# Early queries, keys and biases for the first pair of heads, and reciprocals ahead of the second half of the scores

## The chip, the cores and the metric

The kernel runs on one NeuronCore of one Trainium2 chip. The metric is the device time of one execution in microseconds (us); less is better. The core's engines are TensorE (PE in the profile; its weight loads are PEld), VectorE (DVE), ScalarE (ACT), GpSimd (POOL) and SyncE (SP), which here only issues transfers. Each engine works through its own instructions in order, and they wait for one another through semaphores.

## What is computed

One inference step of a two-layer decoder trunk, for a prompt of 1024 tokens and 8 sample tokens, width 1024. The change touches layer 0 alone: its input projection and the attention behind it.

```python
def even_project(h, pos, w_in, ...):
    z = h @ w_in                      # six sections of 512 columns, and 8 forget logits
    qa, ka = rms_norm(heads(z[..])), rms_norm(heads(z[..]));  va = heads(z[..])
    logf = log_sigmoid(z_forget + b_f)
    qb, kb = partial_rope(rms_norm(..)), partial_rope(rms_norm(..));  vb = heads(z[..])

def fox_block(q, c_q, k, v, c_k):     # group A, 8 heads of 64
    s = q @ k.T * SCALE + (c_q - c_k)     # c = cumsum(logf)
    s = where(pos_k <= pos_q, s, -inf)
    return softmax(s) @ v

# group B, 8 heads: the same over keys at dilations 1, 4, 16, mixed by softmax denominators
# the samples: the same against cached keys, values and log-forgets
# then x += concat(A, B) @ w_out;  x += swiglu(rmsnorm(x));  layer 1 (gated chunk mixing);  x += swiglu(..)
```

## The kernel before, in words

**Projection.** `in_pe` runs `step(i)` for the two head groups i = 0 (A) and i = 1 (B); each has three sections c = 0, 1, 2 for queries, keys and values, and each section nine tiles of tokens (one of 8 sample tokens, eight of 128 prompt tokens). A tile is 24 products of 512 columns into one of three PSUM banks (0 to 2). VectorE scales it out of the bank, and ScalarE's queue stores it to memory (`q_prompt`, `k_prompt`, `v_prompt`; line 739). `step(0)` is written out and `step(1)` stands in a loop of one turn (`peeled_loop`).

**Between.** `forget_pe` (lines 965 to 967) makes the sample tokens' bias sums with three products into banks 2 to 4, and `forget_dve` turns them into `dbias` with a chain of 17 small VectorE operations (lines 945 to 950); it also clears `L`, `Lp` and `Ls` and makes the causal mask tiles `ident16` and `above16`. TensorE and ScalarE wait for the end of that chain (`lg` 14).

**Attention.** The 16 heads are taken as 8 pairs; a pair has 8 units, one for each block of 128 queries, the longest (8 blocks of keys) first: 64 units in all. For each pair, queries and keys come from memory in four parts (`load_qk`, line 997; part n belongs to pair n/4), and TensorE turns each with four 128x128 transposes (`transpose_qk`, line 1229); ScalarE copies even parts and VectorE odd ones to `QT` and `KTr`. The parts of the first pair (n = 0 to 3) are loaded and transposed after the projection, into banks 0 to 3; those of the next pairs within the units before (`QK_AT`), into bank 7.

The order within the attention is written out by hand in `att_pe`, `att_act` and `att_dve`, for u from -2 on. TensorE's turn u is: scores of unit u+2, first half (`scores(u+2, 0)`, line 1246; for group A with two small products of the mask, line 1250); the sums of unit u spread over the rows (`spread_sums`, line 1277, which reads `rl` = 1/l); the product with the values (`window`, line 1293); transposes of the weights of unit u+1 (line 1265), a part of the next pair, scores of u+2, second half, more transposes. VectorE's turn is: bias and minimum of unit u+2's first half (`biased`, line 1453), the output of unit u (`out`, line 1468), one sum of products for the sample tokens (`log_sum`, line 1480), `biased` of the second half, `reciprocals(u+1)` (line 1461), a second `log_sum`. ScalarE takes the exponentials (line 1369) and copies the transposed weights (line 1382).

**The transfer queue.** SyncE issues nearly all loads in one order, in `att_begin_sp` and `att_sp`: parts 0 to 2, `hmask`, `dbias`, part 3, the biases of the first pair (`load_first_bias`), the sample queries `qrep`, six tiles of cached keys `kring`, the values of the first pair `vp`, `own`, then parts 4 to 6. All of them share SBUF with the projection's weight units (`raw`, `Wh`, `Wl`).

The few lines that set this order on SyncE:

```python
sp.wait_ge(z_ps, 2 * NZT)                       # att_begin_sp: the whole projection is done
for j in range(NZ):
    sp.wait_ge(z_out[j], 16 * 2 * NZT // NZ)    # and all of it is stored
for n in range(3):
    load_qk(sp, n)
```

## Time and profile before

| | us |
|---|---|
| median of 3 runs | 2630.19 |
| the runs | 2628.05 to 2633.60 |
| the profiled execution | 2626.38 |
| its span in the profile | 2624.3 |
| TensorE busy, of the span | 2556.8 (97%) |
| VectorE, ScalarE, GpSimd busy | 1133.9, 550.1, 1101.6 |
| last product of the projection starts | 345.83 |
| first scores start | 359.66 |
| last scores biased | 681.12 |

Times within the profile count from the start of its span. The profile gives for each instruction its start and length, and before it the engine's idle time with what ended it; the granted clock of TensorE is given for a stretch, 1.00 for 2.4 GHz and 0.50 for 1.2 GHz. Transfers are listed by their issue and by the time from issue to landing.

### The profile page before, as it was taken

Reading aid. Unit: us, or ns where it says so; the run is one execution under the profiler, and the core shown is the slowest. Engines: PE = TensorE matmul, PEld = TensorE weight load, DVE = VectorE, ACT = ScalarE, POOL = GpSimd, SP = SyncE. Lnnn points to the kernel's source line nnn. Section 1 sums busy time; section 2 is a strip of 40 time slices with the busy share of each in tenths; the row PEclk is TensorE's granted clock in tenths of the full one; section 3 lists DMA queues with packets and bytes.
Section 4 is the critical chain, followed back from the end, with each engine's and each line's share of the span. In section 5 each row is a group of like instructions: output and inputs, shape, how many; then the busy total and the mean of one; then the engine's idle time right before and its main releaser. Section 6 shows DMA issues by size and latency. Waiting matters only on the chain.

```text
span 2624.3 us, 42745 instructions
## 1 busy us (share of the span) xinstructions
PE 2556.8 (97%) x16331; PEld 2344.0 (89%) x16331; DVE 1133.9 (43%) x2258; ACT 550.1 (21%) x1266; POOL 1101.6 (42%) x702
## 2 busy tenths in 40 slices
PE   7999989999999999999999999899999999999999
PEld 5777756666899999999999987899999999999999
DVE  6636536667344333333333360553733333333333
ACT  5201136666322000000000051322300000000001
POOL 4234115566665444333344262435654443333440
PEclk9999999999999999999999999999999999999999
DMA  5223148767312111111111111111121111111111
GB/s 158 70 80 91 60 129 247 217 203 211 96 34 73 49 43 45 44 44 48 48 48 48 33 49 32 49 33 49 33 65 48 44 43 45 43 48 48 48 32 65
DMA packets 218459, 189.83 MB, mean 72 GB/s; under 512 B 29443, under 2 KB 171523, under 8 KB 217956
## 3 DMA queue, kind: packets, MB, share of 16 engines
q1 hardware_dynamic: 200996, 161.89, 21.2%
q10 hardware_dynamic: 17344, 26.35, 2.8%
q8 instruction: 75, 1.23, 0.2%
q14 instruction: 44, 0.36, 0.0%
HBM read 171.19 MB, written 17.01 MB: 72 GB/s over the span
## 4 chain that ended last, share of the span: by engine, by line
PE 69%; DVE 2%; POOL 2%; ACT 1%; issue 1%; ACTq 0%; POOLq 0%; PEldq 0%; DVEq 0%
PE ps L536 63%; PE ps L566 1%; PE ps L568 1%; PE ps L567 1%; ACT ps L2079 1%; POOL Xl L509 1%; POOL Wl L392 1%; POOL Wh L389 1%; DVE hs L479 0%; PE ps L2042 0%; POOL acc_sq L450 0%; PE ps L1265 0%; PE ps L1293 0%; PE ps L2211 0%; DVE VM_EARLY L2163 0%
## 5 line engine op out<-in xcount | busy, mean ns | idle before, releaser
L536 PE MATMUL ps<-Xh,Wh 128*128 128x256 f32 (+2 forms) x2712 | 872.6, 322 | 9.7 <-PE ps L536 3.3
L536 PE MATMUL ps<-Xl,Wh 128*128 128x256 f32 (+2 forms) x2712 | 867.4, 320 | 0.0
L536 PE MATMUL ps<-Xh,Wl 128*128 128x256 f32 (+2 forms) x2712 | 866.4, 319 | 0.0
L389 POOL TENSOR_TENSOR Wh<-raw,zeros 128x1024 fp32r<-128x1024 f32 x178 | 353.9, 1988 | 1072.5 <-PE ps L536 782.4
L536 PEld LDWEIGHTS ps<-Xh,Wh 128*128 128x128 f32 x2712 | 510.3, 188 | 15.6 <-issue 8.8
L536 PEld LDWEIGHTS ps<-Xh,Wl 128*128 128x128 f32 x2712 | 510.9, 188 | 0.0
L536 PEld LDWEIGHTS ps<-Xl,Wh 128*128 128x128 f32 x2712 | 510.3, 188 | 0.7
L392 POOL TENSOR_TENSOR Wl<-raw,Wh 128x1024 fp32r<-128x1024 f32 x178 | 440.9, 2477 | 14.0
L1839 DVE TENSOR_TENSOR Hl<-hf,Hh 128x392 fp32r<-128x392 f32 (+1 forms) x132 | 181.8, 1377 | 464.8 <-ACT Hh L1775 464.8
L536 PE MATMUL ps<-Hh,Wh 128*128 128x392 f32 (+2 forms) x1056 | 340.7, 323 | 1.2 <-DVE xT L1848 1.2
L536 PE MATMUL ps<-Hl,Wh 128*128 128x392 f32 (+2 forms) x1056 | 338.1, 320 | 0.0
L536 PE MATMUL ps<-Hh,Wl 128*128 128x392 f32 (+2 forms) x1056 | 336.8, 319 | 0.0
L1848 DVE TENSOR_TENSOR xT<-ps,xT 128x392 f32<-128x392 f32 (+2 forms) x528 | 263.1, 512 | 163.5 <-PE ps L536 160.6
L1767 ACT ACTIVATE sg<-ps 128x392 f32<-128x392 f32 (+1 forms) x132 | 60.4, 458 | 1062.2 <-PE ps L536 1062.1
L566 PE MATMUL ps<-Wh,Xh 128*128 128x512 f32 x512 | 204.2, 399 | 9.1 <-DVE zt L859 4.0
L1837 DVE TENSOR_TENSOR hf<-ps,sg 128x392 f32<-128x392 f32 (+1 forms) x132 | 67.2, 509 | 320.6 <-PE ps L536 316.5
L568 PE MATMUL ps<-Wh,Xl 128*128 128x512 f32 x512 | 203.2, 397 | 0.0
L567 PE MATMUL ps<-Wl,Xh 128*128 128x512 f32 x512 | 202.8, 396 | 0.0
L536 PEld LDWEIGHTS ps<-Hh,Wh 128*128 128x128 f32 x1056 | 199.0, 188 | 1.7 <-DVE xT L1848 1.4
L536 PEld LDWEIGHTS ps<-Hh,Wl 128*128 128x128 f32 x1056 | 199.5, 189 | 0.0
L536 PEld LDWEIGHTS ps<-Hl,Wh 128*128 128x128 f32 x1056 | 199.5, 189 | 0.0
L1194 POOL TENSOR_TENSOR kring<-kring,qrep 128x512 f32<-128x512 f32 (+1 forms) x96 | 120.6, 1274 | 95.6 <-DMA qrep<-q_sample 60.7
(251 smaller groups left out, 2485.9 us busy)
## 6 DMA issues: line engine op xcount, KB each, us to landing
raw<-in_w_gate_up SPq DMA_DIRECT2D x88, 512.0 KB, 3.8
raw<-in_w_down SPq DMA_DIRECT2D x44, 512.0 KB, 3.5
kring<-in_cache_a_k SPq DMA_DIRECT2D x64, 256.0 KB, 3.6
ring<-in_cache_a_v SPq DMA_DIRECT2D x64, 256.0 KB, 3.1
raw<-in_w_in_even SPq DMA_DIRECT2D x20, 512.0 KB, 4.1
raw<-in_w_in_c SPq DMA_DIRECT2D x16, 512.0 KB, 3.9
xs<-in_x_prompt SPq DMA_DIRECT2D x8, 512.0 KB, 8.5
q_prompt<-zt ACTq DMA_DIRECT2D x16, 256.0 KB, 2.0
```

What stands on the lines that cost most here:

```text
L389: pool.tensor_tensor(h[:, :], r[:, :], zeros[:, :].to_broadcast([P, 1024]), ALU.add).then_inc(split_high, 1)
L392: pool.tensor_tensor(l[:, :], r[:, :], h[:, :].bitcast(F32), ALU.subtract).then_inc(split_done, 1)
L509: eng.tensor_tensor(Xl[:, m, c0:c0 + n], hs[u % NH][:, 0:n], Xh[:, m, c0:c0 + n].bitcast(F32), ALU.subtract).then_inc(s["low_dve" if m % 2 ...
L536: ins = nc.tensor.matmul(out, w, x, start=(j == 0), stop=(j == len(pairs) - 1))
L566: nc.tensor.matmul(out, xh, h, start=begin, stop=False)
L567: nc.tensor.matmul(out, xh, l, start=False, stop=False)
L568: return nc.tensor.matmul(out, xl, h, start=False, stop=end)
L1194: pool.tensor_tensor(keys, keys, qrep[0:r, g, :], ALU.mult).then_inc(prod_done, 1)
L1767: act.activation(sg[:, k % NB, 0:w], ps[:, gate_bank(i, is_last, k), 0:w], ACT.Silu).then_inc(f["silu"].sem, 1)
L1837: dve.tensor_tensor(hf[:, k % NB, 0:w], ps[:, bank, 0:w], sg[:, k % NB, 0:w], ALU.mult).then_inc(f["hid"].sem, 1)
L1839: dve.tensor_tensor(Hl[:, t, c0:c0 + w], hf[:, k % NB, 0:w], Hh[:, t, c0:c0 + w].bitcast(F32), ALU.subtract).then_inc(f["low"].sem, 1)
L1848: dve.tensor_tensor(x, ps[:, jobs.index(("dn", b, m, 0)) % 6, 0:w], x, ALU.add).then_inc(f["dn_add"].sem, 1)
```

## The change

1. **Homes.** `QT` moves to the first raw buffer, parts n = 0 and 1 (`qk_pair`) to the second, and biases, keys, `qrep`, `KTr` and the rest to buffers of split weights that the last section of the projection no longer uses. `bias` has its two halves in two buffers.
2. **The first pair within the projection.** In the last section (i = 1, c = 2), after its tiles 4 to 7, TensorE transposes parts 0 to 3 into banks 3 to 6, and ScalarE and VectorE copy them. SyncE loads parts 0 and 1 as soon as the last keys are stored, then the biases, then parts 2 and 3 as banks are transposed. `step(1)` is written out too, on TensorE, ScalarE and VectorE.
3. **The forget sums.** The three products of `forget_pe` move behind the scores of unit 0, into banks 5 to 7, and VectorE's chain between `biased(1, 0)` and `reciprocals(0)`. `ustr` and `lnd` are made in the last section, the mask tiles right behind the last tile. TensorE's waits for `lg` move to the first places where a bank or `dbias` matters.
4. **The queue.** Behind the projection SyncE issues `hmask`, `dbias`, the values of the first pair, `qrep`, the six keys, `own`, parts 4 to 6.
5. **Reciprocals.** `reciprocals(u + 1)` stands ahead of the first `log_sum` and of `biased(u + 2, 1)`.
6. **The end of the attention.** The raw buffers now hold `QT` and `qk_pair`: of the output projection's weights (units 25 on) only unit 25 is loaded at once, units 26 on after the last scores have been biased.

```diff
@@ homes
+        QT = at_unit("QT", RAW_AT, [P, SEQ])
+        qk_pair = at_unit("qk_pair", RAW_AT + 1, [P, 2, 2 * 2 * P])
...
+        bias = at_unit("bias", HIGH_AT + 2, [P, SPL, SEQ])[:, 0:SPL:SPL - 1, :]
...
@@ in_pe, in_act, in_dve
+        def early_pair(i, c, pos):
+            return pos - 4 if (i, c) == (1, 2) and 4 <= pos < 8 else None
+                        if early_pair(i, c, tt) is not None:
+                            transpose_qk(pe, 0, early_pair(i, c, tt), 3 + early_pair(i, c, tt))
-            peeled_loop(pe, 2, step)
+            for i in range(2):
+                step(i)
...
+                        if early_pair(i, c, pos) in (0, 2):
+                            copy_queries_keys(act, 0, early_pair(i, c, pos), 3 + early_pair(i, c, pos))
...
+                            if (i, pos) == (1, 2):
+                                forget_operands(dve)
+                            if early_pair(i, c, pos) in (1, 3):
+                                copy_queries_keys(dve, 0, early_pair(i, c, pos), 3 + early_pair(i, c, pos))
@@ forget_pe
-            pe.wait_ge(z_free, 2 * NZT)
-            nc.tensor.matmul(ps[:, 2, :], ustr[:, :], flat, start=True, stop=True)
+            nc.tensor.matmul(ps[:, 6, :], ustr[:, :], flat, start=True, stop=True)
...
@@ SyncE
+        def att_early_sp(sp):
+            sp.wait_ge(split_done, 25)
+            for j in range(NZ):
+                sp.wait_ge(z_out[j], 16 * (NZT + 2 * TT) // NZ)
+            for n in range(2):
+                load_qk(sp, n)
+            sp.wait_ge(z_ps, NZT + 2 * TT)
+            sp.wait_ge(c_out, 16)
+            for part in range(3):
+                load_first_bias(sp, part)
+            for n in range(2, 4):
+                load_qk(sp, n)
         def att_begin_sp(sp):
...
-            for n in range(3):
-                load_qk(sp, n)
...
-                load_qk(sp, 3)
                 for part in range(3):
-                    load_first_bias(sp, part)
+                    load_pair_values(sp, 0, part)
                 for g in range(2):
                     load_queries(0, g)
                 for j in range(KR):
                     load_key(0, j)
-                for part in range(3):
-                    load_pair_values(sp, 0, part)
                 own_sp(sp)
@@ att_pe
+                if u == 0:
+                    pe.wait_ge(z_free, 2 * NZT - 1 + c)
...
+                    if y == 1:
+                        pe.wait_ge(lg, 6)
...
-            for g in range(4):
-                transpose_qk(0, g, g)
-            pe.wait_ge(lp_zero, 2)
...
+                if u == -2:
+                    forget_pe(pe)
@@ att_dve
+                if u == -1:
+                    forget_dve(dve)
...
+                reciprocals(u + 1)
                 tiles = log_tiles(u)
                 for sample, tile in tiles[0:1]:
                     log_sum(sample, tile)
                 biased(u + 2, 1)
-                reciprocals(u + 1)
@@ SyncE, behind the attention
-            load_narrow(sp, BASE_OUT, a["w_out_even"][0], 8)
+            load_narrow(sp, BASE_OUT, a["w_out_even"][0], 0, 1)
+            sp.wait_ge(s_biased, 2 * chunk_base[NUNIT])
+            load_narrow(sp, BASE_OUT, a["w_out_even"][0], 1, 8)
```

**TensorE at the end of the projection.** Before, its last product (line 568) is followed by the forget products, the four parts and the first scores:

```order
L89 COMPARE_AND_BRANCH
L965 MATMUL ps<-lfp_56,ustr_199 128x512 [waits z_ps,z_free,lg,lfp_in]
L966 MATMUL ps<-lfp_56,ones_50 128x512
L967 MATMUL ps<-lnd_200,ones_50 128x64
L1229 MATMUL ps<-ident_49,qk0_148 128x128 [waits qk_in0,lg]
L1229 MATMUL ps<-ident_49,qk0_148 128x128 x3
L1229 MATMUL ps<-ident_49,qk1_149 128x128 [waits qk_in1]
...
L1229 MATMUL ps<-ident_49,qk2_179 128x128 [waits qk_in2]
...
L1246 MATMUL ps<-KTr_160,QT_153 128x512 [waits qk_dve,qk_act,lp_zero]
...
L1250 MATMUL ps<-ident16_165,above16_166 128x128 x2
```

With the change each of tiles 4 to 7 has a part behind it (here the last one, part 3, and the first product of tile 8), and behind tile 8 stand the scores at once; the next part (4) keeps its place in unit 0's turn:

```order
L574 MATMUL ps<-Wh0_65,Xl_62 128x512
L1263 MATMUL ps<-ident_49,qk_pair_149 128x128 [waits qk_in0]
L1263 MATMUL ps<-ident_49,qk_pair_149 128x128 x3
L572 MATMUL ps<-Wh3_68,Xh_61 128x512 [waits z_free]
...
L574 MATMUL ps<-Wh0_65,Xl_62 128x512
L1294 MATMUL ps<-KTr_159,QT_148 128x512 [waits z_ps,z_free,qk_dve,qk_act]
...
L1299 MATMUL ps<-ident16_162,above16_163 128x128 [waits lp_zero]
...
L1294 MATMUL ps<-KTr_159,QT_148 128x512 [waits z_free,qk_dve,qk_act]
...
L988 MATMUL ps<-lfp_56,ustr_195 128x512 [waits lg,lfp_in]
L989 MATMUL ps<-lfp_56,ones_50 128x512
L990 MATMUL ps<-lnd_196,ones_50 128x64
L1294 MATMUL ps<-KTr_159,QT_148 128x384 [waits s_biased]
```

What moved: sixteen transposes into the last section, three forget products behind the scores of unit 0.

**SyncE between the projection and the attention** (`kring` are cached keys of the samples, `c_dram` holds the biases). Before:

```order
L997 DMA qk0_148<-q_prompt 128x2x128 [waits z_out1,z_out2,z_out0,z_ps]
L997 DMA qk0_148<-out_k_prompt 128x2x128
...
L1006 DMA hmask_184<-in_c_hmask 128x10
L1007 DMA dbias_182<-in_c_dbias 128x8x32
L997 DMA qk0_148<-q_prompt 128x2x128 [waits qk_ps,c_out]
...
L1102 DMA bias_152<-c_dram 128x2x512
...
L1146 DMA qrep_159<-q_sample 128x512 x2
...
L1090 DMA kring0_150<-in_cache_a_k 128x512
...
L1120 DMA vp_156<-out_v_prompt 128x4x128
...
L1013 DMA own_181<-out_v_sample 8x512 [waits own_zero]
```

With the change, parts 0 to 3 and the biases stand ahead of `hmask`, and the values ahead of the queries and keys:

```order
L1024 DMA qk_pair_149<-q_prompt 128x2x128 [waits z_out1,z_out2,z_out0,split_done]
L1024 DMA qk_pair_149<-out_k_prompt 128x2x128
...
L1140 DMA bias_155<-c_dram 128x2x512 [waits c_out,z_ps]
...
L1024 DMA qk_pair_149<-q_prompt 128x2x128 [waits qk_ps]
...
L1024 DMA qk_pair_149<-q_prompt 128x2x128 [waits qk_ps]
...
L1045 DMA hmask_181<-in_c_hmask 128x10 [waits z_out1,z_out2,z_out0,z_ps]
L1046 DMA dbias_179<-in_c_dbias 128x8x32
L1158 DMA vp_156<-out_v_prompt 128x4x128
...
L1184 DMA qrep_153<-q_sample 128x512 x2
...
L1128 DMA kring_home0_150<-in_cache_a_k 128x512
...
L1051 DMA own_178<-out_v_sample 8x512 [waits own_zero]
```

What moved: 8 loads of parts and 3 of biases to before the projection's end, 3 of values past 2 of `qrep` and 6 of keys; parts 4 to 6 stand last as before.

**VectorE in turn u = 6** (`mx` is the minimum that the exponential waits for). Before:

```order
L1468 TENSOR_TENSOR O2_175<-ps,Rs0_163 128x128 [waits o_low,pv_ps,pt_out]
L1480 TENSOR_REDUCE L_183<-kring0_150 128x8 [waits prod_done]
L1453 ISA S2_00_157,mx_186<-ps,bias_odd_192,mx_tail_187 128x512 [waits pt_ps,s_biased,s_ps,bias_in0]
L1453 ISA mx_186 128x1
L1453 ISA S2_10_158,mx_186<-ps,bias_odd_192,mx_tail_187 128x512 [waits s_biased]
L1453 ISA mx_186 128x1
L1461 RECIPROCAL rl_189<-lsum_188 128x2 [waits p_done]
L1480 TENSOR_REDUCE L_183<-kring1_151 128x8 [waits prod_done]
```

With the change the reciprocal stands ahead of the first sum and of the second half:

```order
L1513 TENSOR_TENSOR O2_172<-ps,Rs0_160 128x128 [waits o_low,pv_ps,pt_out]
L1506 RECIPROCAL rl_186<-lsum_185 128x2 [waits p_done]
L1519 TENSOR_REDUCE L_180<-kring_home0_150 128x8 [waits prod_done]
L1498 ISA S2_00_157,mx_183<-ps,bias_odd_188,mx_tail_184 128x512 [waits pt_ps,s_biased,s_ps,bias_in0]
...
L1498 ISA S2_10_158,mx_183<-ps,bias_odd_188,mx_tail_184 128x512 [waits s_biased]
...
L1519 TENSOR_REDUCE L_180<-kring_home0_150 128x8 [waits prod_done]
```

What moved: the reciprocal past one sum and two operations of line 1453 (line 1498 in the changed kernel).

## Rows read from the trace of the kernel before

**Rows 1.** Stretch: length, busy of PE, PEld, DVE, ACT, POOL, clock, DMA share, GB/s.

```profile
346.20:375.20 29.00, 18.25 (x108) 10.84 (x108) 12.84 (x52) 9.32 (x19) 1.22 (x3) 0.82 0.78 205
```

**Rows 2.** TensorE's timeline, 345 to 376 us: start, length, instruction, idle before.

```profile
345.83 0.39 PE L568 MATMUL ps<-Wh,Xl 128*128 128x512 f32 x1
...
354.27 2.82 PE L1229 MATMUL ps<-ident,qk 128*128 128x128 f32 x12 [4.12 <-DVE acc L950]
...
359.66 2.08 PE L1246 MATMUL ps<-KTr,QT 64*128 64x512 f32 x4
...
372.52 1.97 PE L1293 MATMUL ps<-PT,vp 128*64 128x128 f32 x32 [0.94 <-DMA vp<-out_v_prompt]
...
375.23 0.60 PE L1229 MATMUL ps<-ident,qk 128*128 128x128 f32 x4
```

**Rows 3.** The timeline of SyncE's queue, 349 to 370 us.

```profile
349.41 0.37 SPq L997 DMA_DIRECT2D qk<-q_prompt  x1
...
352.89 0.68 SPq L1007 DMA_DIRECT2D dbias<-in_c_dbias  x1
...
358.16 0.94 SPq L1146 DMA_DIRECT2D qrep<-q_sample  x2
359.89 6.29 SPq L1090 DMA_DIRECT2D kring<-in_cache_a_k  x6
366.22 1.68 SPq L1120 DMA_DIRECT2D vp<-out_v_prompt  x3
...
368.72 0.39 SPq L997 DMA_DIRECT2D qk<-q_prompt  x1
369.15 0.47 SPq L997 DMA_DIRECT2D qk<-out_k_prompt  x1
```

**Rows 4.** TensorE's waits, 366 to 690 us: total, times, longest.

```profile
PE ps L1277 <- DVE rl L1461: 8.5, 12, 2.3
```

**Rows 5.** Timelines of ScalarE's queue and VectorE, 306 to 325 us.

```profile
306.88 0.34 ACTq L739 DMA_DIRECT2D out_k_prompt<-zt  x1
...
324.12 0.75 DVE L841 TENSOR_SCALAR zt<-ps,rstd 128x512 f32<-128x512 f32 x1 [4.63 <-PE ps L568]
```

**Rows 6.** Transfers of key parts, issued 369.1 and 375.8 us on: median us to landing.

```profile
qk<-out_k_prompt SPq DMA_DIRECT2D x1, 128.0 KB, 5.2
...
qk<-out_k_prompt SPq DMA_DIRECT2D x1, 128.0 KB, 2.3
```

**Rows 7.** Stretches, with the columns of rows 1.

```profile
263.90:267.20 3.30, 3.30 (x10) 2.56 (x9) 2.09 (x8) 1.24 (x3) 0.00 (x0) 0.50 0.47 179
...
352.70:362.30 9.60, 6.51 (x24) 4.08 (x26) 2.97 (x13) 1.32 (x4) 0.00 (x0) 0.50 0.76 194
...
365.00:370.00 5.00, 2.82 (x19) 1.90 (x20) 1.76 (x7) 4.25 (x8) 0.00 (x0) 1.00 1.00 349
```

**Rows 8.** VectorE's timeline, 350 to 355 us.

```profile
350.88 0.22 DVE L945 TENSOR_SCALAR acc<-ps 128x64 f32<-128x64 f32 x1
...
354.00 0.21 DVE L950 TENSOR_TENSOR acc<-ps,acc 128x64 f32<-128x64 f32 x1
```

**Rows 9.** Timelines of the three engines around a pair's first unit, 402 to 406 us.

```profile
402.61 1.15 ACT L1369 ACTIVATE S<-S,mx 128x1024 f32<-128x1024 f32 x1 [0.67 <-DVE mx L1453]
...
403.37 0.44 PE L1277 MATMUL ps<-ident,rl 128*64 128x128 f32 x4 [0.68 <-DVE rl L1461]
...
403.96 1.09 PE L1265 MATMUL ps<-ident,S 128*128 128x128 f32 x8
...
404.03 1.14 ACT L1369 ACTIVATE S<-S,mx 128x1024 f32<-128x1024 f32 x1
...
404.93 0.28 DVE L1468 TENSOR_TENSOR O<-ps,Rs 128x128 f32<-128x128 f32 x1
```

**Rows 10.** Timelines of VectorE and GpSimd at the attention's end.

```profile
681.12 0.29 DVE L1453 CUSTOM_DVE_ANT_0 S<-ps,dist 128x128 f32<-128x128 f32 x1
...
689.47 1.90 POOL L389 TENSOR_TENSOR Wh<-raw,zeros 128x1024 fp32r<-128x1024 f32 x1
```

More of the change, by code:

```diff
@@ L234, in build, with at_unit @@
         NO = 4
-        qk = [place(f"qk{j}", [P, 2, 2, P]) for j in range(2)]
-        kring = [place(f"kring{j}", [P, DH]) for j in range(2)]
-        bias_memory = used[0]
-        bias = place("bias", [P, 2, SEQ])
-        QT = place("QT", [P, SEQ])
-        kring += [place(f"kring{j}", [P, DH]) for j in range(2, 4)]
-        vp = place("vp", [P, 8, P])
-        S2 = [[None, None], [None, None]]
-        S2[0][0] = place("S2_00", [P, SEQ])
-        S2[1][0] = place("S2_10", [P, SEQ])
-        qrep = place("qrep", [P, 2, DH])
-        KTr = place("KTr", [P, SEQ])
-        kring += [place(f"kring{j}", [P, DH]) for j in range(4, 6)]
+        def at_unit(name, buffer, shape, dt=F32):
+            return nc.alloc_sbuf_tensor_at(name, shape, dt, offset=(overlay + 31) // 32 * 32 + 4 * 1024 * buffer)
+        RAW_AT, HIGH_AT, LOW_AT = 0, RAW, RAW + SPL
+        QT = at_unit("QT", RAW_AT, [P, SEQ])
+        qk_pair = at_unit("qk_pair", RAW_AT + 1, [P, 2, 2 * 2 * P])
+        qk = [qk_pair[:, j, :].rearrange("p (x t e) -> p x t e", x=2, t=2) for j in range(2)]
+        kring_home = [at_unit(f"kring_home{j}", b, [P, 2, DH]) for j, b in enumerate((HIGH_AT, HIGH_AT + 3, LOW_AT + 3))]
+        kring = [kring_home[j // 2][:, j % 2, :] for j in range(KR)]
+        qrep = at_unit("qrep", HIGH_AT + 1, [P, 2, DH])
+        dist = at_unit("dist", HIGH_AT + 2, [P, SEQ])
+        bias = at_unit("bias", HIGH_AT + 2, [P, SPL, SEQ])[:, 0:SPL:SPL - 1, :]
+        assert HIGH_AT + 2 + SPL - 1 == LOW_AT + 1
+        vp = at_unit("vp", HIGH_AT + 4, [P, 8, P])
+        S2 = [[None, None], [None, None]]
+        S2[0][0] = at_unit("S2_00", HIGH_AT + 5, [P, SEQ])
+        S2[1][0] = at_unit("S2_10", LOW_AT, [P, SEQ])
+        KTr = at_unit("KTr", LOW_AT + 2, [P, SEQ])
+        used[0] = (overlay + 31) // 32 * 32 + 4 * 1024 * (LOW_AT + 4)
         Rs = [place(f"Rs{j}", [P, P]) for j in range(2)]
@@ L251, in build @@
         used[0] += 4 * P
-        score_memory = used[0]
         S2[0][1] = place("S2_01", [P, SEQ - P])
@@ L256, in build @@
         O = [place(f"O{j}", [P, P]) for j in range(NO)]
+        mv_memory = used[0]
         MV = place("MV", [P, DH])
         vx = place("vx", [P, 2, P])
-        qk.append(place("qk2", [P, 2, 2, P]))
+        qk.append(place("qk2", [P, 2, 2, P])[:, :, :, :])
         ring = place("ring", [P, SLOTS, DH])
@@ L282, in build @@
         assert used[0] <= lfp_end
-        used[0] = score_memory
+        used[0] = mv_memory
         ustr = place("ustr", [P, P])
@@ L337, in load_wide, with load_narrow @@
                 load_unit(sp, base + j, j + (base % SPL if isinstance(base, int) else 0), rows(w, 2 * j, 2, col, DH), 2)
-        def load_narrow(sp, base, w, count):
-            for m in range(count):
+        def load_narrow(sp, base, w, first, end):
+            for m in range(first, end):
                 load_unit(sp, base + m, base + m, rows(w, 0, KT, m * P, P), KT)
@@ L810, in in_act @@
             input_square(act, 2)
-            peeled_loop(act, 2, step)
+            for i in range(2):
+                step(i)
         def in_dve(dve):
@@ L880, in in_dve @@
             input_low(dve, 1)
-            peeled_loop(dve, 2, step)
+            for i in range(2):
+                step(i)
         lg, lg_a = sem("lg"), sem("lg_a")
@@ L951, in forget_dve @@
             dve.wait_ge(lg, n)
+            dve.wait_ge(lf_out, 32)
+            dve.memset(Lp[:, :, :], 0.0).then_inc(lp_zero, 1)
+            dve.memset(L[:, :, :], 0.0)
+            dve.memset(Ls[:, :], 1.0)
         def forget_act(act):
@@ L996, in load_qk @@
                 for x, src in enumerate((q_prompt, a["k_prompt"])):
-                    sp.dma_start(qk[n % 3][:, x, :, :], src[grp, rows, cols].rearrange("(t p) e -> p t e", p=P)).then_inc(qk_in[n % 3], 16)
+                    sp.dma_start(queries_keys(n)[:, x, :, :], src[grp, rows, cols].rearrange("(t p) e -> p t e", p=P)).then_inc(qk_in[n % 3], 16)
+        def att_early_sp(sp):
[10 more added lines that the diff above has]
+                load_qk(sp, n)
         def att_begin_sp(sp):
@@ L1546, in after_window @@
                     gathered(sample_at(w, VALUES_AT + 2), w)
-            for g in (1, 3):
-                copy_queries_keys(0, g, g)
-            dve.wait_ge(att_const_in, 32)
             for u in range(-2, NUNIT):
```

99 lines of the change are left out of this document (49 added, 50 removed).

## The prediction

> **What bounds the kernel now.** I read the profile from the whole to the seam. TensorE is busy nearly all of the span, so only a stretch in which it stands still, or runs at half its clock, can give time back. The table of stretches shows one: from the end of the projection to the fifth part's transposes it is busy 18.25 of 29.0 us, at a mean clock of 0.82 [rows 1]. TensorE's timeline shows what stands there [rows 2]. The last product ends at 345.83 + 0.39 = 346.2. The transposes of the first parts begin at 354.27, after 4.12 us without work, and the first scores only at 359.66. At 372.52 the values of the first pair were late by 0.94 us. At 375.23 come the transposes of part 4, and from there on TensorE's waits are few. So 375.23 is my landmark: how much earlier it comes is the gain at the seam. SyncE's queue shows what is behind it [rows 3]: nothing of the attention is issued before 349.41, when the last store has landed. Then SyncE needs until 369 for everything up to part 4. Within the attention the largest of TensorE's waits is for the reciprocals, 12 times, 8.5 us together [rows 4]. That wait is what the change's second half is about.
>
> **The first pair within the projection.** Removed from the seam are sixteen transposes, their loads, the copies and the biases. They cost TensorE something in the last section, which it fills without a gap. Twelve of them took 2.82 us at half clock [rows 2, 7], so four would take 0.47 at full clock, and four within the attention 0.60 [rows 2]. I take 0.53 for each part, 2.1 us for four, with bounds 1.9 and 2.4. The projection then ends at 346.2 + 2.1 = 348.3. Are the parts there in time? The last keys' store is issued at 306.88 and the fifth tile is scaled from 324.12 on [rows 5]. That leaves 17 us for a store and for a load that lands within 5.2 us [rows 6]. Parts 2 and 3 are issued when parts 0 and 1 are transposed and are wanted two tiles later, some 11 us, since VectorE's row for a tile is 0.75 long behind 4.63 of waiting; that suffices too. The copies lie beside projection tiles, on engines that wait for them. Writing out `step(1)` removes a few register and branch instructions from engines of which TensorE shows no idle time there: nothing.
>
> **The landmark without a late transfer.** From the first scores to the landmark took 375.23 - 359.66 = 15.6 us, of which 0.9 was the wait for the values. With the scores starting at 348.3 that puts it at about 363. The forget sums now lie in this stretch: 3 products, and on VectorE the chain from 350.88 to 354.21, 3.3 us [rows 8], ahead of the second half of unit 1. That half used to wait for TensorE for about as long, and the first scores save about 1 us at full clock. I let these cancel. If they don't, the next paragraph hides them: it is later than 363 in any case.
>
> **What is late next: part 4.** SyncE issues the loads of part 4 behind the values, `qrep` and six keys, as before, and the only thing that has left the queue ahead of them is what now comes early. Counted from the projection's end: the last store lands after 349.41 - 346.2 = 3.2 us; `hmask` and `dbias` take 1.2 (the row of `dbias` ends at 353.57, and 0.5 more is `hmask`), `qrep` 359.89 - 358.16 = 1.7, the keys 366.22 - 359.89 = 6.3, values and `own` together 368.72 - 366.22 = 2.5, and the key half of part 4 is issued 0.4 later [rows 3]. That is 15.3. Such a transfer took 5.2 us to land where 1 MB of biases and all the keys were queued before it, and 2.3 on a quiet queue [rows 6]. The biases are gone, and keys are issued at 256 KB in 1.05 us, 250 GB/s, where the queues moved 349 [rows 7]. So I take 3.0, near the lower end. Part 4 is there at 348.3 + 15.3 + 3.0 = 366.6, and TensorE, ready at 363, waits some 3.7 us for it. The seam gives 375.23 - 366.6 = **8.6 us**, where without that wait it would give 12. By the fit of 2.0 us plus bytes over 436 GB/s in the Trainium skill (DMA: Bandwidth & Descriptors, Anatomy of one DMA), made for another issuing path, my estimate is 2.3 us for these 128 KB; the gain would be 0.7 larger. The quiet row agrees with it and the loaded row does not, which is why I go by the rows.
>
> **The clock.** After a wait of 1.9 us in the projection TensorE worked 3.3 us at 0.50 [rows 7]; work of 3.3 us at half clock is worth 1.6. After the long wait at the seam now it was 9.6 us at 0.50 with 6.5 busy, a loss of 3.3, and a stretch of 5 us that was busy for 2.82 kept 1.00 [rows 7]. A new wait of 3.7 us is nearest to the first in what follows it, dense work: I take a loss of **1.6**, between 0 and 3.3.
>
> **The reciprocals.** The wait of 0.68 at 403.37 is typical: `rl` was late because VectorE biased the second half first. With `rl` early TensorE goes on 0.7 sooner, but its next work but one, the transposes at 403.96, needs the exponential that started at 402.61, right behind VectorE's minimum, and takes until about 403.85 with its readout [rows 9]. So the wait moves one step down, from `rl` to the exponential. On VectorE the same work stands ahead of that minimum, plus a reciprocal of 0.16, which at eight pair starts may cost 1.3 us. The two longest waits (2.3 the longest [rows 4]) have the same end: VectorE was waiting there for GpSimd's product, and the minimum waits for it still. A few small waits in other units remain as gain. I take **0.3** together, between -1.3 and 8.5.
>
> **The end of the attention.** Unit 26 is loaded once the last scores are biased, at 681.4, and GpSimd splits it only at 689.47, behind its own last outputs [rows 10]. That leaves 8 us for a transfer: nothing. If it were late, its split and then TensorE would be late by what is missing.
>
> **Sum.** 8.6 - 1.6 + 0.3 = 7.3 us less. Against the profiled execution of 2626.38 that is 2619.1; the median of the runs shown stands 3.8 higher at 2630.19, and what is timed is compared with it: **2622.9 us**.
>
> **Rivals.**
> - *The reciprocals pay.* If the moved waits find work that is ready, up to all 8.5 us come on top of 7.0: 2630.2 - 15.5 = 2614.7 at best, 2618 with half of it. For it: 12 waits on just this operation. Against it: the exponential in rows 9 ends 0.1 us before TensorE wants it. Chance 0.12.
> - *The queue is as full as before.* Then part 4 takes 5.2 us to land (2.2 more) and the clock costs 3.3: 8.6 - 2.2 - 3.3 + 0.3 = 3.4 us, 2626.8, no difference that can be told. For it: values and `qrep`, 1 MB, are issued within 3.5 us right ahead of the keys. Against it: the biases' 1 MB is gone. Chance 0.21.
> - *The reciprocal blocks VectorE: slower.* It waits for the exponential of the second head. At 404.03 + 1.14 and its readout this ends at about 405.3, while the output ahead of it starts at 404.93 and is over by 405.2 [rows 9]: everything behind it, the second half's bias and the sums of the samples, would stand for 0.1 to 0.3 us. If that happened in every unit at 0.3, and TensorE felt it, it would be 64 x 0.3 = 19 us, less 7.0: 12 slower, 2642. It decides from 0.11 us a unit on. Against it: the row is of a pair's first unit, where the window is shortest and the exponential longest; elsewhere the window covers the exponential. A wait at the head of VectorE's queue holds all behind it by the Trainium skill too (TensorE: Matmul & The Clock Gate, Architectural detail: strictly first in, first out). Chance 0.05.
> - *The change does not do what it says:* the order of instructions shows that it does; what could fail is only the timing of the early loads, for which there are 17 us.
>
> **How the numbers follow.** The measurement can tell about 0.2%, 5.3 us, from no change. My forecast, a gain of 5.3 to 9, has a chance of 0.6; its own range is 2620 to 2625. With the first rival that makes 0.71 for faster. The second rival and the forecast's lower edge make 0.24 for no difference, the third 0.05. The range from 2616.5 to 2627.5 reaches from half of the first rival to the second, and leaves out the slower case.
>
> **What would show it.** Right: the first scores within 0.5 us of the projection's end, four transposes behind each of tiles 4 to 7 with no wait for `qk`; a wait of 3 to 5 us ahead of the transposes of part 4 with the transfer of `qk` as what ended it, the clock at 0.50 for some us behind it; TensorE's wait for `rl` nearly gone, and in its place waits for exponentials (line 1369 now) of about the same sum. Wrong: part 4 in time (gain near 12), waits for `rl` gone and none in their place, VectorE waiting for exponentials at each reciprocal, or GpSimd waiting for the weights of unit 26.

## The result, and the profile after

| | kernel before | changed kernel |
|---|---|---|
| median of 5 runs | 2630.21 us (2628.05 to 2633.6) | 2618.39 us (2611.99 to 2618.64) |
| profiled execution | 2626.38 us, span 2624.3 | 2618.45 us, span 2616.6 |
| granted clock, mean of the profiled execution | 0.992 | 0.994 |

The ratio is 0.9947, with a 95% interval from 0.9932 to 0.9961. The changed kernel is faster by 11.8 us between the medians (13.9 by the ratio). I had forecast 7.3. The time lies inside the range, near its fast edge; the gain is over half as large again as I said. Between the two profiled executions it is 7.9 us.

**The seam.** TensorE's timeline of the changed kernel, 345.5 to 372 us: start, length, instruction, idle before.

```profile
346.27 0.39 PE L574 MATMUL ps<-Wh,Xl 128*128 128x512 f32 x1
346.96 1.13 PE L1294 MATMUL ps<-KTr,QT 64*128 64x512 f32 x4 [0.30 <-PE ps L574]
...
353.98 0.65 PE L1316 MATMUL ps<-ident,S 128*128 128x128 f32 x4 [0.83 <-DVE acc L964]
...
359.93 0.98 PE L1316 MATMUL ps<-ident,S 128*128 128x128 f32 x7
365.86 1.11 PE L1263 MATMUL ps<-ident,qk_pair 128*128 128x128 f32 x4 [4.95 <-DMA qk_pair<-out_k_prompt]
366.90 2.08 PE L1294 MATMUL ps<-KTr,QT 64*128 64x512 f32 x4
368.91 1.75 PE L1316 MATMUL ps<-ident,S 128*128 128x128 f32 x7
```

The first scores follow the projection's last product after 0.30 us, where 13 us lay between them before [rows 2]. Then all is dense until 360.9, but for 0.83 at 353.98 and 0.25 at 357.81. There TensorE stands 4.95 us for part 4, the wait that the prediction named. Behind it four transposes take 1.11 instead of 0.60, four scores 2.08 instead of 1.13: it works at half its clock.

The stretches of the changed kernel, columns as in rows 1: from the last product to part 4, behind part 4, and the place in the projection that rows 7 show at 0.50 before.

```profile
346.66:365.86 19.20, 12.87 (x91) 7.20 (x92) 10.89 (x47) 9.13 (x16) 4.38 (x6) 0.98 0.73 198
364.90:371.70 6.80, 5.84 (x23) 3.25 (x23) 1.43 (x4) 2.25 (x5) 0.00 (x0) 0.51 0.31 87
258.00:270.00 12.00, 10.14 (x45) 7.93 (x44) 10.10 (x22) 2.26 (x5) 2.67 (x2) 1.00 0.39 116
```

The same twelve microseconds of the projection in the kernel before:

```profile
258.00:270.00 12.00, 10.15 (x38) 7.86 (x37) 10.11 (x22) 2.25 (x5) 2.46 (x1) 0.86 0.36 110
```

In front of the seam nothing differs but this: the same busy time, once at 1.00 and once at 0.86 in the mean, which is 1.7 us. The change does not touch that place, and this difference is chance: in a second profiled execution of each kernel it is the other way round, 1.00 before and 0.86 with the change (the same window of before_again and of after_again):

```profile
258.00:270.00 12.00, 10.07 (x44) 7.85 (x43) 10.11 (x22) 2.25 (x5) 2.47 (x1) 1.00 0.37 110
258.00:270.00 12.00, 10.07 (x37) 7.75 (x36) 10.14 (x18) 2.25 (x5) 3.77 (x2) 0.86 0.48 131
```

Of the 14 profiled executions of this study eight have 0.86 there and six 1.00.

The timeline of SyncE's queue in the changed kernel, 345 to 372 us:

```profile
349.83 0.34 SPq L1045 DMA_DIRECT2D hmask<-in_c_hmask  x1
...
351.06 1.71 SPq L1158 DMA_DIRECT2D vp<-out_v_prompt  x3
352.81 0.94 SPq L1184 DMA_DIRECT2D qrep<-q_sample  x2
354.56 5.82 SPq L1128 DMA_DIRECT2D kring_home<-in_cache_a_k  x6
...
361.16 0.40 SPq L1024 DMA_DIRECT2D qk_pair<-q_prompt  x1
361.60 0.47 SPq L1024 DMA_DIRECT2D qk_pair<-out_k_prompt  x1
```

The key half of part 4 is issued 14.9 us behind the projection's end (346.66) and is there 4.3 us later, at 365.86.

**The attention.** TensorE's waits of the changed kernel, 346 to 700 us: total, times, longest.

```profile
PE ps L1316 <- ACT S L1421: 5.2, 6, 2.2
PE ps L1263 <- DMA qk_pair<-out_k_prompt: 5.0, 1, 5.0
...
PE ps L1350 <- DVE Lm L1532: 2.1, 2, 1.4
...
PE ps L1328 <- DVE rl L1506: 0.6, 2, 0.3
```

The wait for `rl` is down from 8.5 us in 12 places [rows 4] to 0.6 in 2, and waits for exponentials (`S`) of 5.2 stand in its place; before there was one of 2.4, at the seam. At the pair's first unit, which is that of rows 9, it looks like this (timelines of ScalarE and of TensorE, 394 to 400 us):

```profile
395.83 1.15 ACT L1421 ACTIVATE S<-S,mx 128x1024 f32<-128x1024 f32 x1 [0.72 <-DVE mx L1498]
```

```profile
395.78 0.44 PE L1328 MATMUL ps<-ident,rl 128*64 128x128 f32 x4
...
397.12 1.09 PE L1316 MATMUL ps<-ident,S 128*128 128x128 f32 x8 [0.69 <-ACT S L1421]
```

The 0.68 has moved one step down, as 0.69. The transposes start at 397.12 and before at 403.96: 6.84 us have been won by here. The last wait of the attention, 0.30 us ahead of a product of the output projection, ends at 687.93 now and at 697.06 before, 9.13 earlier. So the rest of the attention adds 2.3 us. Behind it the difference falls to 7.7 at the span's end, over stretches at half clock that lie elsewhere in the two executions.

### The profile page after: what moved, and what is told of

The parts are those of the page before. It is cut to its first block, busy times and chain, and to the rows that moved or that the text cites. A ratio compares the mean times of both kernels' runs of the same rounds, so it can differ in the third digit from the quotient of the medians.

```text
span 2616.6 us, 42737 instructions
## 1 busy us (share of the span) xinstructions
PE 2554.6 (98%) x16331; PEld 2341.8 (89%) x16331; DVE 1130.3 (43%) x2258; ACT 551.1 (21%) x1266; POOL 1100.8 (42%) x702
## 4 chain that ended last, share of the span: by engine, by line
PE 71%; DVE 2%; POOL 2%; ACT 1%; issue 1%; DMA 0%; SPq 0%; ACTq 0%; POOLq 0%; PEldq 0%; DVEq 0%
PE ps L542 64%; PE ps L572 1%; PE ps L574 1%; PE ps L573 1%; PE ps L1294 1%; PE ps L1316 1%; PE ps L1346 1%; ACT ps L2119 1%; POOL Xl L515 1%; POOL Wl L398 1%; POOL Wh L395 1%; DVE hs L485 0%; PE ps L2082 0%; POOL acc_sq L456 0%; PE ps L1384 0%
## 5 line engine op out<-in xcount | busy, mean ns | idle before, releaser
L1229 POOL TENSOR_TENSOR kring_home<-kring_home,qrep 128x512 f32<-128x512 f32 (+1 forms) x96 | 120.6, 1273 | 95.1 <-DMA qrep<-q_sample 63.1
```

The costliest lines, as they stand in the source:

```text
L1229: pool.tensor_tensor(keys, keys, qrep[0:r, g, :], ALU.mult).then_inc(prod_done, 1)
```

## The experiments

Twelve runs were made, ten with an edit and two of the kernels as they stand. Each median stands beside that of the kernel before on the same chip in the same hour; a ratio of 0.001 is 2.6 us.

| run | median us | before | ratio, 95% interval |
|---|---|---|---|
| after_again | 2616.95 | 2630.17 | 0.9950 (0.9937 to 0.9964) |
| recip_back | 2620.67 | 2630.17 | 0.9966 (0.9952 to 0.9979) |
| recip_only | 2624.15 | 2630.17 | 0.9980 (0.9971 to 0.9989) |
| part4_early | 2609.96 | 2630.17 | 0.9922 (0.9909 to 0.9936) |
| loops_only | 2629.76 | 2630.10 | 1.0001 (0.9992 to 1.0010) |
| forget_first | 2615.33 | 2630.10 | 0.9943 (0.9929 to 0.9956) |
| sums_behind | 2605.62 | 2630.10 | 0.9910 (0.9896 to 0.9923) |
| forget_first_queue | 2614.96 | 2628.60 | 0.9945 (0.9932 to 0.9959) |
| recip_starts | 2615.51 | 2628.60 | 0.9946 (0.9932 to 0.9959) |
| sums_behind_recip_back | 2610.74 | 2628.60 | 0.9929 (0.9916 to 0.9943) |
| values_behind | 2617.24 | 2628.39 | 0.9962 (0.9948 to 0.9975) |
| before_again (one execution) | 2626.35 | | |

### What the reciprocals give

**recip_only** is the kernel before with one line moved:

```
                 if u >= 0 and QK_AT.get(j) in (1, 3) and it < PAIRS - 1:
                     copy_queries_keys(it + 1, QK_AT[j], 7)
+                reciprocals(u + 1)
                 tiles = log_tiles(u)
...
                 biased(u + 2, 1)
-                reciprocals(u + 1)
```

> The kernel before with only the reciprocals moved ahead of the second half of scores. Theory: 2 to 3 us faster than before, at the same first landmark (part 4's transposes at about 375 us), the waits for rl gone and those for exponentials in their place. Rival: within 0.5 us of before. If it is faster by 5 us or more, the first pair's part of the change gave less than its landmark says.

It is 6.0 us faster than before, twenty times the 0.3 that I had put down for this part. **recip_back** is the changed kernel with the opposite edit.

> The changed kernel with the reciprocals of 1/l back behind the second half of scores, everything else kept. Theory (the 2.3 us that the attention gained behind the first pair are the reciprocals' doing): 2 to 3 us slower than the changed kernel, the waits of TensorE for rl back to 8 to 9 us, and those for the exponential shorter. Rival 1 (my prediction's term): 0.3 us slower, the same within what is measured. Rival 2 (the gain behind the first pair is the clock's and the keys' order): no slower at all.

It is 3.7 us slower than the changed kernel beside it (2616.95). Both went the theory's way, and beyond its 2 to 3 us; the rival that stood for my own term fell. The 6.0 of recip_only met the condition that would have made the first pair's part smaller than its landmark, and that conclusion does not hold: recip_back, which is that part alone, is 9.5 us faster than before. The two parts overlap. Alone they give 6.0 and 9.5, together 13.2, and the 2.3 between are near the 2.1 us by which the early reciprocals lengthen the wait for part 4 (below). TensorE's waits, 346 to 700 us, of recip_only:

```profile
PE ps L1265 <- ACT S L1369: 7.3, 6, 2.6
...
PE ps L1297 <- DVE Lm L1491: 2.1, 2, 1.4
...
PE ps L1277 <- DVE rl L1461: 0.5, 2, 0.3
```

and of recip_back:

```profile
PE ps L1328 <- DVE rl L1506: 10.6, 13, 2.2
PE ps L1263 <- DMA qk_pair<-out_k_prompt: 2.9, 1, 2.9
...
PE ps L1350 <- DVE Lm L1532: 1.0, 2, 0.6
```

Before, the waits for `rl`, `S` and `Lm` made 8.5 + 2.4 + 1.0 = 11.9; in recip_only they make 0.5 + 7.3 + 2.1 = 9.9. Another 0.8, waits of the `rl` transposes for ScalarE's copy in the same view of before, is gone as well: 2.8 us less. With the change it is 10.6 + 1.0 + 0.8 = 12.4 against 0.6 + 5.2 + 2.1 = 7.9, of which 2.1 only come back in the wait for part 4 (5.0 for 2.9): 2.4 less. So the waits account for 2.4 to 2.8 us of the 3.7 to 6.0.

The longer waits for `Lm` are moved waits too. In the kernel before TensorE waits 0.68 for `rl` at 484.40 and 0.62 for `Lm` at 485.68, in recip_only 1.38 for `Lm` alone at 487.20; at the other place 0.23 and 0.40 became 0.70. Each time some 0.07 us is new.

Where I went wrong shows at one of the pairs' starts. Timelines of ScalarE and TensorE of the kernel before, 646 to 653 us:

```profile
649.42 1.15 ACT L1369 ACTIVATE S<-S,mx 128x1024 f32<-128x1024 f32 x1 [1.39 <-DVE mx L1453]
650.47 0.18 ACT L1369 ACTIVATION_READ_ACCUMULATOR S<-S,mx 128x1 f32 x1
```

```profile
650.18 0.44 PE L1277 MATMUL ps<-ident,rl 128*64 128x128 f32 x4 [1.63 <-DVE rl L1461]
650.45 0.39 PE L1293 MATMUL ps<-PT,vp 128*64 128x128 f32 x4
650.77 1.05 PE L1313 MATMUL ps<-hmask,MV 128*128 128x2 f32 x8
651.68 1.07 PE L1265 MATMUL ps<-ident,S 128*128 128x128 f32 x8
```

and TensorE at the same place of recip_only:

```profile
648.73 0.44 PE L1277 MATMUL ps<-ident,rl 128*64 128x128 f32 x4
648.99 0.39 PE L1293 MATMUL ps<-PT,vp 128*64 128x128 f32 x4
649.31 1.05 PE L1313 MATMUL ps<-hmask,MV 128*128 128x2 f32 x8
651.01 1.09 PE L1265 MATMUL ps<-ident,S 128*128 128x128 f32 x8 [0.64 <-ACT S L1369]
```

Here eight products of a sample (0.9 us) stand between the window and the transposes. So before, the exponential was over at 650.65, 1.03 us ahead of the transposes at 651.68. With `rl` early TensorE does those products while the exponential runs, and 1.63 of waiting becomes 0.64, 0.99 less. At rows 9 only the sums and the window, 0.59 us, stand there; the exponential was over 0.11 ahead of the transposes, and the wait stayed (0.68, 0.69). At the longest wait, 2.30 at 566.38, it was over at 566.85 for transposes at 566.96, and 2.38 is left. So what can be won at a place is the time by which the next thing waited for was already there. I had read the case of rows 9 and laid it on all the others.

**recip_starts** keeps the reciprocals early only around a pair's start:

```
+                if u % 8 in (6, 7):
+                    reciprocals(u + 1)
                 tiles = log_tiles(u)
...
                 biased(u + 2, 1)
+                if u % 8 not in (6, 7):
+                    reciprocals(u + 1)
```

> The changed kernel with the reciprocals ahead of the second half only in the two units around each pair's start, and behind it in the other six. Theory (at a pair's start the wait moves from rl to the exponential and little is gained; the gain of the reciprocals sits in the waits of 0.2 to 0.8 us of the other units and in the one of 1.63 at 650): it keeps a third to a half of the 3.4 us, 2618.5 to 2620 us. Rival (the gain is at the pair's starts): 2617 us, the same as the changed kernel.

2615.51 us, ratio 0.9946: nothing is lost, which is for the rival; the interval, to 0.9959, does not quite shut out the theory's near edge. TensorE's waits, 346 to 700 us:

```profile
PE ps L1316 <- ACT S L1421: 4.7, 5, 2.3
...
PE ps L1350 <- DVE Lm L1532: 1.8, 2, 1.4
PE ps L1328 <- DVE rl L1506: 1.3, 5, 0.3
```

With 0.8 for ScalarE's copy that makes 8.6, where recip_back has 12.4 and the changed kernel 7.9. So 3.8 of the 4.5 us are kept at the pairs' starts, the wait of 1.63 among them (it is 0.65 here); I had counted that one to the other units. The 0.7 of the others is less than the medians can tell. Its profiled execution is the slowest of its five (2620.50), and shows the gain in the waits only.

**sums_behind_recip_back** asks the same of the fastest kernel (below), with `reciprocals(u + 1)` behind `biased(u + 2, 1)`.

> The kernel of sums_behind (part 4 early, the first sum behind the second half's bias) with the reciprocals behind that bias, too. Theory (a reciprocal behind the second half is late by that bias alone, 1.5 to 2.2 us, whatever the sums do): 2 to 4 us slower than sums_behind, 2608 to 2609.5 us. Rival (it was late because of the sum that stood ahead of the bias): within 1 us of 2605.6.

5.1 us slower than sums_behind between the medians (5.0 by the ratios), more than expected; the rival fell. TensorE waits 5.6 us for `rl` there, in 9 places, though no sum stands ahead of the bias: the bias alone makes it late.

### The queue at the seam

**part4_early** moves part 4 ahead of the repeated queries and the keys in SyncE's queue:

```
                     load_pair_values(sp, 0, part)
+                load_qk(sp, 4)
                 for g in range(2):
                     load_queries(0, g)
...
-                for n in range(4, 7):
+                for n in range(5, 7):
```

> The changed kernel with one line moved: the two transfers of part 4 are issued behind the first pair's values and ahead of the repeated queries and the six keys. Theory (the 4.95 us wait at 360.9 and the 6.8 us at half clock behind it are the queue's alone): the wait for qk_pair is gone, the first scores of unit 3 come 5 to 8 us earlier, 2611 to 2614 us. Rival (the wait is handed on: to part 5 and 6, to the keys' sums on VectorE or to the splits of GpSimd): the same landmark comes earlier, but the time is within 2 us of the changed kernel.

7.0 us faster than the changed kernel, ratio 0.9922; the theory stands, 1 us beyond its range. TensorE's timeline, 345 to 385 us:

```profile
361.41 0.98 PE L1317 MATMUL ps<-ident,S 128*128 128x128 f32 x7
362.23 0.60 PE L1264 MATMUL ps<-ident,qk_pair 128*128 128x128 f32 x4
362.75 1.13 PE L1295 MATMUL ps<-KTr,QT 64*128 64x512 f32 x4
```

The wait of 4.95 is gone, and the rows behind it have their full-clock lengths (0.60, 1.13). At 395 the kernel is 6.3 us ahead of the changed one, though its projection ended 1.5 us later: 7.8 us for one line. Part 4's transposes come at 362.23, where the prediction had TensorE ready at 363, and 13.0 us earlier than before, where it had 12 "without that wait". But 1.7 us of it were handed on, as the rival had it. The timelines of TensorE, VectorE and GpSimd around 550 us:

```profile
554.06 1.56 PE L1317 MATMUL ps<-ident,S 128*128 128x128 f32 x8 [3.93 <-ACT S L1422]
```

```profile
551.38 0.69 DVE L1520 TENSOR_REDUCE L<-kring_home 128x8 f32<-128x512 f32 x1 [3.04 <-POOL kring_home L1230]
```

```profile
550.09 2.48 POOL L1230 TENSOR_TENSOR kring_home<-kring_home,qrep 128x512 f32<-128x512 f32 x2 [10.79 <-DMA qrep<-q_sample]
```

The repeated queries land late, GpSimd's product follows, VectorE stands 3.04 us for its sum over it, and the bias of the second half is queued behind that sum: TensorE waits 3.93, where it waited 2.25 at that place in the changed kernel (its longest in the waits above).

**sums_behind** takes up that chain, on top of part4_early:

```
                 tiles = log_tiles(u)
-                for sample, tile in tiles[0:1]:
-                    log_sum(sample, tile)
                 biased(u + 2, 1)
+                for sample, tile in tiles[0:1]:
+                    log_sum(sample, tile)
```

> The kernel with part 4 issued early, with the first sum over a key tile moved on VectorE behind the bias of the second half of scores, in every unit. Theory (the longest waits for the exponential at a pair's start, 3.9 us at 554, come from VectorE standing 3.0 us for GpSimd's product, which waits for the repeated queries, with the second half of scores queued behind it): that wait goes, and 2 to 5 us with it, 2605 to 2608 us. Rival (the sums are then late for the samples' logits, and the key slots come free later): the waits for Lm and MV grow by as much, and the time is the same or worse.

2605.62 us, 4.3 less than part4_early. The place of the 3.93 (TensorE's timeline, 544 to 556 us):

```profile
549.83 1.09 PE L1317 MATMUL ps<-ident,S 128*128 128x128 f32 x8 [0.45 <-ACT S L1422]
```

TensorE's waits for exponentials fall from 6.4 to 1.5 us, those for `Lm` grow only from 2.1 to 2.3. This is the fastest kernel of the study: 24.5 us under before, ratio 0.9910.

**values_behind** issues the first pair's values behind the keys, as before the change.

```
-                for part in range(3):
-                    load_pair_values(sp, 0, part)
                 for g in range(2):
                     load_queries(0, g)
                 for j in range(KR):
                     load_key(0, j)
+                for part in range(3):
+                    load_pair_values(sp, 0, part)
```

> The changed kernel with the first pair's values issued behind the six keys again, as before the change; part 4 keeps its place behind both. Theory (values that are issued at some 359 us land at about 364, and the first window wants them at 358): TensorE waits 5 to 7 us for vp at the first window, the wait for part 4 shrinks to nothing, and the window's work of some 3 us that used to lie ahead of that wait comes behind it: 2 to 4 us slower than the changed kernel, 2619 to 2621 us. Rival (the wait only changes its name, since part 4 ends it at the same time): within 1 us of 2617.3.

Two rows of TensorE's timeline, 345 to 380 us:

```profile
363.76 3.68 PE L1346 MATMUL ps<-PT,vp 128*64 128x128 f32 x32 [5.92 <-DMA vp<-out_v_prompt]
...
368.63 0.60 PE L1263 MATMUL ps<-ident,qk_pair 128*128 128x128 f32 x4
```

The wait is there as expected (5.92 for `vp`, none for part 4), but at 397 us this execution is only 0.07 behind the changed kernel's, 0.5 if the 0.4 by which its projection ended earlier is set against it. The median of 2617.24 says the same. The ratios, 0.9962 against 0.9947 and 0.9950, would make it 3 to 4 us slower, with intervals that overlap. The trace is for the rival, the times leave it open. (The profiled execution, 2615.32, is its fastest of five.)

### The forget sums, and the written-out loop

**forget_first** puts the forget sums ahead of the first scores on both engines, on top of part4_early (in short; the engine waits for `qk_act` and `qk_dve` to be 2 ahead of them):

```
-                if u == -2:
-                    forget_pe(pe)
...
+            forget_pe(pe)
             for u in range(-2, NUNIT):
...
-                biased(u + 2, 0)
-                if u == -1:
+                if u == -2:
                     forget_dve(dve)
+                biased(u + 2, 0)
```

> The kernel with part 4 issued early (label part4_early), with the forget sums ahead of the first scores on TensorE and VectorE again, as before the change. Theory (their place among the scores is worth something only because nothing else is late there): the first scores' bias waits for VectorE's chain of 3.3 us, TensorE stands some 3 us ahead of the first transposes of weights, and may lose 1.6 us to the clock behind it: 2 to 5 us slower than part4_early. Rival (they cancel, as the prediction had it): within 1 us.

5.4 us slower than part4_early: the theory stands, just beyond its 5 us. The row, and the one behind it (timeline of TensorE, 347 to 370 us):

```profile
356.05 1.65 PE L1295 MATMUL ps<-KTr,QT 64*128 64x384 f32 x4 [2.96 <-DVE mx_tail L1500]
```

2.96 us of waiting, and 1.65 for scores that take 0.92 at the full clock. **forget_first_queue** makes the same edit in the changed kernel, where part 4 is late.

> The changed kernel (part 4 queued behind the keys, as the change has it) with the forget sums ahead of the first scores again. With part 4 early the same edit cost 5.4 us (2615.33 against 2609.96), a wait of 2.96 us and more time at half clock. Theory (in the changed kernel the wait for part 4 covers their place, as the prediction had it): the wait for qk_pair shrinks from 4.95 to about 2 us, unit 3's scores come at the same time, and the time is within 1.5 us of the changed kernel, 2616 to 2619 us. Rival: the cost is the same as without that wait, 2620 us or more.

2614.96 us, ratio 0.9945, the same as the changed kernel's 0.9947 and 0.9950; by the ratios the theory stands for the time. Its seam, TensorE's timeline, 347 to 370 us:

```profile
355.92 1.65 PE L1294 MATMUL ps<-KTr,QT 64*128 64x384 f32 x4 [2.96 <-DVE mx_tail L1499]
...
366.84 0.60 PE L1263 MATMUL ps<-ident,qk_pair 128*128 128x128 f32 x4
```

The wait for part 4 has not shrunk to 2 us but is gone: TensorE comes 2.96 us of waiting and some 3 of half clock later, and part 4 is there. So in the change as it stands the new place of the forget sums is worth nothing that can be told; with part 4 early it is worth 5.4. Two covers lie over one another, and each edit pays only once the other is made. In turn, with the sums first, it makes no difference where part 4 is queued (2615.33 and 2614.96).

**loops_only** is the kernel before with `peeled_loop(..., 2, step)` replaced by `for i in range(2): step(i)` on TensorE, ScalarE and VectorE.

> The kernel before with the in-projection's section written out for the second pass on TensorE, ScalarE and VectorE, as the change has it, and nothing else. Theory (writing it out costs and gains nothing): within 1.5 us of before. Rival (part of the gain, and the half clock that the first profile shows after 263 us, come from the loop): 2 us faster or more.

Ratio 1.0001: nothing, as expected.

### The same kernels once more

> The changed kernel once more, unchanged. Theory (the gain of the medians exceeds that of the two profiled executions because executions differ by their stretches at half clock, and the one profiled execution of before was among its better ones): the five times spread again over some 5 us or more, and lower times go with a higher mean clock: 0.003 more clock is worth some 6 to 8 us. Rival (the spread comes from transfers or from something else of the run): the times differ at the same clock. The ratio to before should come out between 0.993 and 0.997 again.

> The kernel before, unchanged, for a second profile. Theory (the profiled execution that the prediction stood on was among the better ones, 2626.38 against a median of 2630.2, by its clock): this one is nearer to 2630, with the same waits of TensorE within the attention (rl 8 to 9 us) and more time at half clock than the 41.7 us of the first profile. Rival: same time at half clock, and the difference lies in waits for transfers.

after_again has its ratio where it was expected, and in both kernels lower times go with a higher clock. before_again fell: not nearer to 2630, and at 0.993 with less half clock, not more.

The ten times of the changed kernel run from 2611.99 to 2618.64 at mean clocks of 0.993 to 0.997, and the lowest has the 0.997. Of the kernel before, 48 executions on several chips are listed with their clock. They average 2631.3 us at 0.990 (4 of them), 2629.9 at 0.991 (22), 2628.5 at 0.992 (16) and 2627.1 at 0.993 (6): 1.4 us for each thousandth. Its mean is 0.9915, that of the changed kernel's ten is 0.9941. By that slope the clock stands for 3.6 us of the gain between the medians. The second profiled execution of before took 2626.35 us, not the 2630 expected, with 8.6 us of waits for `rl`. Both profiled ones stand at the low edge of that kernel's times. For their clocks, 0.992 and 0.993, they are 2.1 and 0.8 us below the averages. Why is open.

## Why the prediction was half right

- **The projection takes the four parts for 2.1 us: right.** Four transposes of 0.60 each stand at 322.53, 328.53, 334.52 and 340.51, none with a wait. It ends at 346.66 against 346.22; with the 1.7 us that the execution before lost at half clock at 264 and this one did not, that is 2.1.
- **Transfers of parts 0 to 3, biases: in time, as said.** TensorE's first wait for another engine behind the projection is the 0.83 at 353.98.
- **TensorE ready 14.7 us behind the projection's end: right.** It is 14.3 (360.91).
- **Part 4 at 18.3: right.** In the changed kernel's profile it is 19.2: the issue came 14.9 behind the end for 15.3, but the landing took 4.3 for the 3.0 that I chose "near the lower end" of 2.3 to 5.2. The biases are gone, but 2.6 MB of values, repeated queries and keys stand ahead of it, and a key tile takes 6.1 us in the median to land, so that most of them are still under way. In three more executions (after_again, recip_back, recip_starts) it landed in 3.4 to 3.5 us, and was there 18.2 to 18.5 behind the end. The Trainium skill's fit (DMA: Bandwidth & Descriptors, Anatomy of one DMA), made for transfers that GpSimd issues, gives an estimate of 2.3 us for these 128 KB; none of these four traces agrees with it.
- **The clock, −1.6 (0 to 3.3): the mechanism right, the size within its spread.** 5.84 us of work at 0.51 behind the wait is a loss of 2.9. I had gone by the stretch behind a wait of 1.9 us, and the wait was 4.95. Ten microseconds around the same place show 8.36 of work at 0.66 in after_again (wait 4.06), a loss of 2.8, but 8.79 at 0.83 in recip_starts (wait 3.94), which is 1.5.
- **The seam, 8.6 − 1.6 = 7.0: 6.8 in the traces, by luck as near as that.** Part 4 came 0.9 later and the clock cost 1.3 more than said, and the 1.7 us upstream, which are chance, cover most of both. More executions say the same without that luck: the landmark of rows 9 stands at 403.96, 404.15, 406.06 and 406.18 in the four with the old seam (before, before_again, recip_only, loops_only) and at 397.12 and 399.02 in the two of the changed kernel, 7.0 between the means. But between the medians recip_back, which is this part alone, is 9.5 us faster than before. The 2.5 beyond 7.0 do not show in these landmarks, and their cause is open.
- **The reciprocals, 0.3: the step that failed.** "So the wait moves one step down" holds, 0.68 to 0.69. "The two longest waits have the same end" holds for that of 2.30 at 566, and not for that of 1.63 at 650, which became 0.64: VectorE does not wait for GpSimd there, and the exponential was over 1.03 us before TensorE came to it. The step took the margin of rows 9, 0.1 us, for that of every place. VectorE's cost, said to be up to 1.3 us, hardly shows: the waits for `Lm` grow from 1.0 to 2.1, but 0.9 of that are moved waits for `rl`. The waits fall by 2.4 to 2.8 us, and the medians by 3.7 to 6.0. The first rival, to which I gave 0.12, had this mechanism, though at most 2.8 of its 8.5 us of waits went away. That its 2618 came out (2618.39) is partly luck: half of 8.5 on top of 7.0 is 2619.0, and the seam's medians gave 2.5 us of it.
- **The carry-over to the median** took the 3.8 us between before's profiled execution and its median as a constant. The changed kernel's profiled execution is at its own median (2618.45 and 2618.39). So 3.9 us of the gain between the medians are not in the two traces at all.

- **Slips in the sums.** Besides that 2618, a gain of 9 is 2621.2 where the forecast's own range says 2620, and 0.6 and 0.12 make 0.72, not 0.71. Nothing hangs on them.

Together: in the runs beside one another, 13.2 us (2616.95 against 2630.17) are 9.5 of the seam, for which I had 7.0, and 3.7 of the reciprocals on top of it, for which I had 0.3. In the traces less is seen: 7.3 forecast and 2.1 to 2.5 more in the waits for the reciprocals make 9.4 to 9.8; 11.8 were measured in the first comparison. The rest of 2.0 to 2.4 is less than the clock's share of 3.6, but that share is a correlation over executions and was not produced by an edit. It was not tried whether the shorter waits are what raised the clock. At one place the traces speak against it. recip_back has a wait of 1.62 at 642.68 and work at 0.50 from 644.2 to 647.4, and the changed kernel has 0.65 there and none. But the kernel before has 1.63 at 650.18 and none either, and recip_starts has the same 0.65 as the changed kernel and works at half clock behind it:

```profile
643.41 1.97 PE L1316 MATMUL ps<-ident,S 128*128 128x128 f32 x8 [0.65 <-ACT S L1421]
```

The eight transposes take 1.09 in the changed kernel. The cause of this rest stays open.

## What to carry to other kernels

A wait that moves one step down is worth the margin by which the next thing waited for was there before: 0.11 us at one pair's start, 1.03 at another. Work between the two places makes the margin, if it keeps the engine beyond that moment. Read it at each place where the wait occurs, not at one that looks typical. When a seam closes, ask which transfer is queued last among those that the new order wants first; here one line in SyncE's queue was worth 7.0 us, as much as the seam's whole forecast. And two edits that are each hidden by the other's delay have to be tried together: the later forget sums alone and the earlier part 4 alone gave nothing, and both gave 5.0 us between the medians (2614.96 to 2609.96), 6 by the ratios.

## What was not expected of the hardware

- A stretch at half clock can add more than half to the price of a wait: 4.95 us of waiting for part 4 and 2.9 lost behind it came back together in part4_early, as 7.8 at the landmark. But the same idle in the projection, 1.85 us at 263, was followed by 0.50 in one execution and by 1.00 in the other, and at a pair's start a wait of 0.65 was followed by half clock in recip_starts and not in the changed kernel; one profile does not tell which.
- The same 128 KB of keys landed in 2.3, 5.2 [rows 6] and 4.3 us in three surroundings of one queue, and in 3.4 in another execution of the third.
- The times of one unchanged kernel lie up to 8.8 us apart (2624.78 to 2633.60), and its two profiled executions 3.8 below its median. A gain read off two profiled executions is uncertain by as much as this change's smaller half.
